# Products with 512 moved columns: one output tile after the other, or both tiles in turns in two PSUM banks

## What is computed

```python
# first block, each of 2 layers (FFN_DIM = 2816)
up = causal_dwconv(h @ ffn_w_up[layer], ffn_conv_w[layer], ffn_conv_b[layer])
gate, val = jnp.split(up, 2, axis=-1)
x = x + (jax.nn.silu(gate) * val) @ ffn_w_down[layer]
# second block, each of 2 layers (D_FF = 2816, ATTN_WIDTH = 1536)
u, q, k, v, g_pool, g_attn = jnp.split(xn @ w_in, SPLITS, axis=-1)
...
a, gval = jnp.split(xn @ w_up, 2, axis=-1)
```

## Time and profile before

| what | value |
|---|---|
| median of 3 runs | 1823.73 us (1823.53 to 1823.83) |
| profiled execution, from its first to its last instruction (the span) | 1822.0 us |
| TensorE busy | 1809.9 us, 99% of the span |
| VectorE busy | 1387.2 us, 76% |
| ScalarE busy | 1045.9 us, 57% |
| groups of form D | 96, of 32 matmuls each |

### The profile page before, as it was taken

One profiled execution on the slowest core, in us unless ns is written; L12 is line 12 of the kernel. 1 busy time (PEld: TensorE's weight loads), 2 busy tenths in 40 slices (PEclk: granted clock), 3 DMA queues, 4 the chain that ended last, 5 costly groups with the idle time before them and its releaser, 6 DMA issues.

```text
span 1822.0 us, 26151 instructions
## 1 busy us (share of the span) xinstructions
PE 1809.9 (99%) x10278; PEld 1572.7 (86%) x10278; DVE 1387.2 (76%) x2044; ACT 1045.9 (57%) x1287; POOL 18.8 (1%) x45
## 2 busy tenths in 40 slices
PE   8999999999999999999999999999999999999998
PEld 8898889888988888988889888898889888889887
DVE  7968887997696887799867756679857765578974
ACT  6667646775565774577644456555544446556553
POOL 1000000000000000000000000000000000000000
PEclk9999999999999999999999999999999999999999
DMA  9976555655887665555555565555556565555553
GB/s 229 199 162 153 174 184 190 198 188 181 183 163 158 161 181 173 174 185 185 187 187 191 176 183 190 178 170 187 187 183 195 176 196 186 173 183 186 186 176 104
DMA packets 254962, 328.01 MB, mean 180 GB/s; under 512 B 25909, under 2 KB 169537, under 8 KB 254841
## 3 DMA queue, kind: packets, MB, share of 16 engines
q1 hardware_dynamic: 254576, 326.00, 61.2%
q10 hardware_dynamic: 264, 0.35, 0.1%
HBM read 325.23 MB, written 1.09 MB: 179 GB/s over the span
## 4 chain that ended last, share of the span: by engine, by line
PE 85%; DVE 9%; DVEq 3%; issue 1%; DMA 0%; ACT 0%; SPq 0%; ACTq 0%
PE psum L719 16%; PE psum L655 15%; PE psum L657 15%; PE psum L656 15%; PE psum L643 8%; PE psum L721 7%; PE psum L740 3%; DVEq L1568 3%; DVE w_low L411 2%; DVE w_low L415 2%; DVE tmp L1689 1%; PE psum L718 1%; DVE xbc L1689 1%; PE psum L842 1%; DVE tmp L1597 1%
## 5 line engine op out<-in xcount | busy, mean ns | idle before, releaser
L423 ACT ACTIVATE w_hi<-w_raw 128x2048 fp32r<-128x2048 f32 (+2 forms) x309 | 574.2, 1859 | 286.2 <-PE psum L657 261.7
L411 DVE TENSOR_TENSOR w_low<-w_raw,w_hi 128x1024 fp32r<-128x1024 f32 (+1 forms) x310 | 375.3, 1211 | 239.3 <-ACT w_hi L423 231.9
L719 PE MATMUL psum<-act,w_hi 128*128 128x512 f32 x1536 | 528.1, 398 | 0.0
L655 PE MATMUL psum<-w_hi,act 128*128 128x512 f32 x1248 | 492.4, 395 | 0.3 <-DVE w_low L411 0.3
L657 PE MATMUL psum<-w_hi,act 128*128 128x512 f32 x1248 | 486.4, 390 | 0.0
L656 PE MATMUL psum<-w_low,act 128*128 128x512 f32 x1248 | 486.0, 389 | 0.0
L721 PE MATMUL psum<-act,w_low 128*128 128x256 f32 x1344 | 377.1, 281 | 0.0
L415 DVE TENSOR_TENSOR w_low<-w_raw,w_hi 128x1024 fp32r<-128x1024 f32 (+2 forms) x307 | 361.1, 1176 | 0.0
L719 PEld LDWEIGHTS psum<-act,w_hi 128*128 128x128 f32 x1536 | 276.0, 188 | 52.5
L657 PEld LDWEIGHTS psum<-w_hi,act 128*128 128x128 f32 x1248 | 234.2, 188 | 49.4
L655 PEld LDWEIGHTS psum<-w_hi,act 128*128 128x128 f32 x1248 | 234.5, 188 | 47.9 <-DVE w_low L411 1.5
(11 more groups left out here) (290 smaller groups left out, 1678.4 us busy)
## 6 DMA issues: line engine op xcount, KB each, us to landing
w_raw<-in_w_in SPq DMA_DIRECT2D x121, 1024.0 KB, 6.0
w_raw<-in_ffn_w_up SPq DMA_DIRECT2D x40, 1024.0 KB, 5.1
w_raw<-in_w_up SPq DMA_DIRECT2D x40, 1024.0 KB, 5.1
w_raw<-in_ffn_w_down SPq DMA_DIRECT2D x16, 1024.0 KB, 5.1
w_raw<-in_w_down SPq DMA_DIRECT2D x16, 1024.0 KB, 5.0
w_raw<-in_w_branch_b SPq DMA_DIRECT2D x8, 1024.0 KB, 5.0
w_raw<-in_w_out SPq DMA_DIRECT2D x8, 1024.0 KB, 5.0
w_raw<-in_w_a SPq DMA_DIRECT2D x8, 1024.0 KB, 5.7
```

The lines of the kernel that those rows point to most:

```text
L411: dve.tensor_tensor(lo[:, 0:cut, :], of[:, 0:cut, :], hi[:, 0:cut, :], ALU.subtract).then_inc(w_lo_front, 1)
L423: act.activation(group_view(whi, q % HIGH, g), group_view(raw, q % LOW, g), ACT.Copy).then_inc(w_hi, 1)
L655: mm(o, xh, hi[:, k, :], start=g["opens"] and k == 0, stop=False)
L719: last = mm(o, wh, both[:, g["tile"] + k, :, :], start=k == 0, stop=end, skip_group_check=True)
```

## The change

In `proj_double` both banks are waited for ahead of the first matmul. Then k runs outside and t inside: for each k two matmuls on high weights (512 columns), tile 0 in the first bank and tile 1 in the second, then two on low weights (256 columns), in the same two banks. The number of matmuls, of loads of a held tile and of columns is as before. `first_tile` is raised by the last matmul but one of the group, `group_done` by the last. The wait for the back half of the low weights stands ahead of k = 4 for both tiles.

```diff
                 proj_waits(b, i, n, G)
-                for t in range(TT):
-                    if t == 1:
-                        bank_wait(b, i, n, g["banks"][1])
-                    o = PJ[:, g["banks"][t], :].rearrange("p (a t) -> p a t", a=2)
-                    for k in range(g["kt"]):
-                        if t == 0 and k == FRONT[g["kt"]]:
-                            pe.wait_ge(w_lo_back, q + 1)
-                        end = k == g["kt"] - 1
-                        wh, wl = hi[:, k, t * P:(t + 1) * P], lo[:, k, t * P:(t + 1) * P]
-                        if end:
-                            mm(o[:, 1, :], wl, ahi[:, g["tile"] + k, :], start=False, stop=False, skip_group_check=True)
-                        last = mm(o, wh, both[:, g["tile"] + k, :, :], start=k == 0, stop=end, skip_group_check=True)
-                        if not end:
-                            mm(o[:, 1, :], wl, ahi[:, g["tile"] + k, :], start=False, stop=False, skip_group_check=True)
-                    if t == 0:
-                        last.then_inc(step("first_tile"), 1)
+                bank_wait(b, i, n, g["banks"][1])
+                sums = [PJ[:, bank, :].rearrange("p (a t) -> p a t", a=2) for bank in g["banks"]]
+                for k in range(g["kt"]):
+                    if k == FRONT[g["kt"]]:
+                        pe.wait_ge(w_lo_back, q + 1)
+                    for t in range(TT):
+                        mm(sums[t], hi[:, k, t * P:(t + 1) * P], both[:, g["tile"] + k, :, :], start=k == 0, stop=False, skip_group_check=True)
+                    for t in range(TT):
+                        last = mm(sums[t][:, 1, :], lo[:, k, t * P:(t + 1) * P], ahi[:, g["tile"] + k, :], start=False, stop=k == g["kt"] - 1,
+                                  skip_group_check=True)
+                        if t == 0 and k == g["kt"] - 1:
+                            last.then_inc(step("first_tile"), 1)
                 last.then_inc(group_done, 1)
```

## The result

The changed kernel takes 1845.62 us (median of 4 runs, 1845.45 to 1845.78) against 1823.68: ratio 1.012, 95% interval 1.0108 to 1.0132. It is slower by 21.9 us; the prediction was 21.1 us slower, 1844.8. The span of the profiled execution grows by 21.4 us, from 1822.0 to 1843.4; the prediction had 1843.1. The median lies 2.2 us above that span now and lay 1.7 above it before, so half a microsecond of the 21.9 comes from which execution was profiled.

The account below looks back on a forecast made before the run. TensorE, busy 99% of the span at full clock, was taken to bound the kernel. Stops +23.5 and pace -2.4 gave +21.1 us on the 1822.0 span, 1843.1, so a median of 1844.8 us; range 1838 to 1853.

Parts of the forecast that it names:

- The mechanism, the place and the count of the stops: Q and K phase: TensorE stands for the just-filled bank until copy and addition are done, 22 times, +23.5 us.
- The length of a stop: Q1 to K5: from R through copy, addition and restart, 1.07 us a stop.
- The first three steps: At a stop: tile 0's last matmul ends at R + 0.04, copy starts at R + 0.08, addition at R + 0.50.
- R: The time at which the next group would start without a stop; the steps of a stop are counted from it.
- the restart: TensorE after VectorE's release: load 0.04 later, first matmul 0.10 above the pace; together 0.15 us.
- The pace: Q and K groups and second block's UP: new order gives back 0.04 us in each of 60 groups, -2.4 us.
- if the loss goes with these changes of width: Group pace: 0.09 us lost at 512-to-256 changes; these fall from 14 to 8, so 0.04 us comes back.
- The first block's UP phases: VectorE is slower than TensorE there, so the pace gain doesn't count; DN3's waits grow from 0.4 to about 1.1 us.
- VectorE late: Rival, Q and K: pooling sums delay the addition, 16 stops cost 1.52 us each; 1852 us, chance 0.14.
- Overhead taken away by banks in turns: Rival, all 60 counting groups: alternate banks give 5.12 us a group, 0.52 less; 1816 us, chance 0.03.
- The lost clock: Rival, Q and K: stops drop TensorE's clock to 1.2 GHz, +135 us, about 1980 us, chance 0.02.

Follow-up runs that it names:

- Runs of eight: Seven banks in Q and K; tile after tile, all eight 512-column matmuls, then all eight of 256, against the changed kernel's order; 5.587 us a group, 1820.96 us.
- pace_runs_of_2: Seven banks in Q and K; tile after tile, two 512-column matmuls then two of 256, without the changed kernel's bank change; 5.573 us a group, 1820.61 us.
- pace_other_bank: Seven banks in Q and K; against the changed kernel, widths in turns, each 256 in the other bank than the 512 ahead; 5.653 us a group, 1824.67 us.
- pace_same_bank: Seven banks; against the changed kernel, widths in turns, a tile's 512 and 256 in one bank, tiles in turns; 5.653 us a group, one phase 5.547; 1823.17 us.
- turns_up_block1: The kernel before with the new order in the first block's UP groups alone (36 of 96); 1823.94 us, ratio 0.9999.
- wait_in_front: The kernel before, tile after tile, with only the wait for the second bank moved ahead of the group; 1835.98 us, ratio 1.0065.
- seven_banks: The changed kernel with seven banks instead of three in the Q and K phase's ring; 1820.1 us, ratio 0.9978 against the kernel before.
- four_banks: The changed kernel with four banks instead of three in the Q and K phase's ring; 1820.38 us, ratio 0.998.

## Why the prediction was right

- **The mechanism, the place and the count of the stops**: as forecast, 22, at the groups Q1 to K5, by VectorE's addition behind ScalarE's copy. The records give 0.9 us a wait for the matmul (20.0 us in 22) and 1.1 for the load, where some 0.8 was forecast. Four banks remove them all.
- **The length of a stop**: 1.07 was forecast, 1.16 measured. The first three steps fit within 0.01 (copy at R + 0.09 against 0.08, addition at 0.50 against 0.50). The term that was too small is the restart: TensorE's load came 0.12 behind the addition's recorded end (986.79 + 0.42 = 987.21, load at 987.33) where the row of line 411 had 0.04, and the first matmul 0.03 behind the load where it had 0.01. The group that followed needed 0.09 more than an undisturbed one (its first matmul 0.306 instead of 0.233 us), where 0.10 was counted. 22 x 0.09 = 2 us too little. The trace shows where the load lost time: for a bank TensorE's queue has a waiting instruction of its own (line 626), recorded at 987.26, 0.04 behind the addition's end, and the load follows 0.08 after its start. In the earlier trace rows the load itself carries the wait, and comes 0.04 behind.
- **The pace**: 0.04 back was forecast, 0.067 measured, so the term took 60 x 0.027 = 1.6 us too little off. The range of the term held it, but its reason did not: the step "if the loss goes with these changes of width" failed. Runs of eight lose 0.04 with two changes from 512 to 256, the changed kernel 0.026 with eight, and one order of matmuls loses nothing in one phase and 0.106 in another. The prediction also looked for the loss at the 256 behind a 512; the trace has it at the matmuls of 512. In the two pairs of orders that were compared the bank doesn't matter, on which I had been undecided: pace_runs_of_2 against the changed kernel, and pace_other_bank against the slow phases of pace_same_bank.
- These two errors are of opposite sign and nearly equal: 25.5 - 4.0 = 21.5 instead of 23.5 - 2.4 = 21.1. That the total fits better than its terms is luck.
- **The first block's UP phases**: nothing was gained there, as turns_up_block1 shows. DN3's wait in layer 0 grew from 0.40 to 1.46 us, in the changed kernel too; about 1.1 was forecast, with the smaller gain in pace.
- **VectorE late** (the rival at 1852, first in the prediction's list): it did not come. At each of the 22 stops VectorE waited for the copy, 0.24 us at the least, where 0.3 was forecast. wait_in_front shows what it looks like where it does come.
- **Overhead taken away by banks in turns** (1816): falls. It needed 5.12 us a group, and no order went below 5.547, the sum of the paces of its widths.
- **The lost clock**: falls, the granted clock is full through 22 gaps of 1 us.
- The Trainium skill, page "TensorE: Matmul & The Clock Gate", section "Back-to-back issue gap", gives for a single matmul at full clock a gap of its columns / 2.4 + 2.5 ns. An estimate from that formula is 16 x (0.216 + 0.109) = 5.20 us a group in any order. Here six orders of the same matmuls gave 5.547 to 5.653 us, 7 to 9% above it and up to 2% apart, so the measurement decides against the formula for this stream. The Trainium skill, page "Perfetto Trace Analysis", section "Matmuls", asks that groups rotate through banks so that one is emptied under the next; seven_banks and four_banks agree, 1820 against 1845.6 us.

**What stays open** is why the pace depends on the order. The one fast phase of pace_same_bank began with a first matmul of 0.255 us and its slow ones with 0.233 or 0.243, so the way into a phase may decide; that is not shown, since nothing here changes the start of a phase by a known small time. This would be the next test.

## What to carry to other kernels

When products of several output tiles are interleaved, the first tile is complete at the end of the group instead of in the middle. Count the banks again: here, with two a group, three in the ring are one too few and four are enough, and a stop costs the whole chain of copy, addition and restart (1.16 us here). And ask of each gain in pace whether the engine behind is already the bound there: the faster pace of 36 of the 96 groups was worth nothing.

## What the runs showed that was not expected

- The same order of matmuls in the same kernel runs at 5.547 or at 5.653 us a group in the mean, phase by phase, at full granted clock; within a phase the pattern repeats and stays.
- The restart behind a wait for a bank is slower than behind a wait for low weights: the load of the held operand comes 0.12 us behind the addition's end, against 0.04 behind the low weights' front half. The first matmul of 512 columns is slow behind both, 0.306 and 0.33 us instead of 0.233.
